# A hybrid attention block on one core: 128-row products in attention, a re-ordered start, and the last normalising turn inside the merge stage

## The chip, the cores and the metric

The kernel runs on one core of one Trainium2 chip. The metric is the device time of one execution in microseconds (us), lower is better. The core has five engines with a queue of their own each: TensorE (PE, with its weight loads as PEld), VectorE (DVE), ScalarE (ACT), GpSimd (POOL) and SyncE (SP); here SP issues most transfers. They wait for each other through semaphores.

## The reference: what is computed

A residual block over 2048 tokens of width 1024. A combined projection of the normalised input gives queries, keys, values and gates of two attention branches: FoX, 8 heads of 64, causal, with a cumulated forget term, and SWA, 8 query and 2 key heads in a sliding window with a distance penalty and a sink. Their outputs are gated, projected, merged and projected again.

```python
h = _rms_norm(x, norm_g[layer]) * (1.0 + scale[:, None, :]) + shift[:, None, :]
proj = h @ w_in[layer]
...
logits = logits + F[:, :, qs:qe, None] - F[:, :, None, :qe]
...
p = jax.nn.softmax(logits, axis=-1).astype(v.dtype)
...
logits = logits - slopes[:, :, None, None] * dist
...
p = jax.nn.softmax(jnp.concatenate([logits, sink], axis=-1), axis=-1)[..., :WK]
...
ya = (ya * jax.nn.silu(za)) @ w_o_fox[layer]
...
yb = (yb * jax.nn.silu(zb)) @ w_o_swa[layer]

merged = jax.nn.sigmoid(ga) * ya + jax.nn.sigmoid(gb) * yb
x = x + gate[:, None, :] * (merged @ w_out[layer])
```

The first two logits lines are FoX, the next two SWA.

## The kernel before

Five stages follow each other, each a block at whose end the engines meet: condition and norm, `project` (its last product ends near 1102 us), `attention` (to 1737 us), `merge` and `output`. Operands are held as a high and a low part, so that most products come as three.

**Attention** is a list of 350 steps, worked out before the kernel is built. A step is one 128-key tile of a FoX block (512 queries of a head; 32 blocks) or one part of an SWA unit (a tile of 128 queries, 4 heads; 32 units): part A over the current keys, part B over the 64 before them. `units` says how many SWA units stand inside each FoX block. In step n TensorE works on row maxima (`row_max`), then on the scores of step n+3 (`score`), then on the product of step n with the values (`gather`). ScalarE takes the exponential of the scores and casts it to its high part Ph, GpSimd subtracts for the low part Pl.

- FoX scores: L1266 multiplies Ka and Qa over HD + 4 = 68 rows (64 of the head, two for the forget term, two for the row maximum), L1267 the pair tiles Kb, Qb over 128 rows.
- `row_max` finds the shift of the softmax beforehand. For FoX it is L1028 (66 rows). For SWA L1037 puts the distance penalty (biasM) into the bank, and two products L1039 add QBa and KBa over HD = 64 rows; VectorE takes the maximum (L1095). Four such sets belong to one SWA tile; there are 16 tiles. The maxima go through a transpose and copies to two rows of Qa or QBa (`move_row`).
- SWA part B: L1277 and L1278 score, L1279 adds biasB over 64 rows, and L1307, L1308 and L1311 multiply Ph and Pl with VB over 64 rows.
- At its end each block is multiplied by its gate Z into yT (`collect`); the sums of the softmax go to memory (`copy_sums`), and eight turns read a group of them back, invert, store, load the inverses spread over all rows into R, and scale yT in four operations (`invert`, `scale`). The eighth turn comes behind the last step, in the `TAIL` of 28 empty steps.

**What sets the order.** `timed` gives each row maximum a due step, at least `TILE_LEAD` = 16 steps ahead of its block, and `at` the step in which it stands. `k_due`, `q_due`, `s_due` and `z_due` give the step at which SP issues the loads of keys, queries, SWA tiles and gates. SP works through its list in order: an entry that waits holds all behind it. `START` is -3. The maxima of the first three blocks are already made at the end of `project`. `tables` makes the 24 pieces of the bias tables on ScalarE in six steps from `TABLES_AT`; `set_up` fills constants on VectorE before its first step.

**Merge.** `split_rows` loads eight weight rows (512 KB each), ScalarE makes their high part (woh) and VectorE the low part (wol). yT is split in blocks of 256 tokens: ScalarE yh, GpSimd yl. TensorE's first product waits for the first block of yl and the first weight row, and VectorE gates the outputs with tiles of 1 MB each (`load_gates`).

## Time and profile before

| | us |
|---|---|
| time, median of 3 runs | 2129.09 (2123.26 to 2143.35) |
| the profiled execution | 2127.95 |
| its span, first to last instruction | 2126.2 |
| TensorE busy | 1979.7 (93%) |
| VectorE busy | 885.6 (42%) |
| ScalarE busy | 737.5 (35%) |
| GpSimd busy | 550.5 (26%) |

"Busy" of TensorE is the time in which a product is under way by the profile. Neighbouring products overlap there, so how fast TensorE works is read from the distance between starts. The granted clock is 1.00 at 2.4 GHz and 0.50 at 1.2 GHz; its mean over the span is 0.962.

### The profile page before, as it was taken

The numbers are of one execution on the slowest core, as the hardware profiler recorded it, in microseconds if no ns is written. First come the engines' busy times: TensorE is split into PE (matmuls) and PEld (weight loads), VectorE is DVE, ScalarE is ACT, GpSimd is POOL, SyncE is SP. The second block draws the span as 40 slices with busy tenths as digits, with TensorE's granted clock in tenths as the row PEclk, the third lists the DMA queues.
The fourth block names the chain that finished last, engine by engine and source line by source line (L and its number), as shares of the span: only waits on it lengthen the run. The fifth ranks groups of instructions, "written<-read, shape, count | busy, mean of one in ns | idle before, by whom it ended". The sixth has DMA issues, their size and how long they took to land. (4 is left out here: it accounts for less than half of the span.)

```text
span 2126.2 us, 27983 instructions
## 1 busy us (share of the span) xinstructions
PE 1979.7 (93%) x9722; PEld 1555.5 (73%) x9722; DVE 885.6 (42%) x1851; ACT 737.5 (35%) x1375; POOL 550.5 (26%) x502
## 2 busy tenths in 40 slices
PE   7389999999999999999989899999999959998998
PEld 2368778798788788888866566666666639997887
DVE  2945555562212220000234455555565335554332
ACT  2622222220112132121115677767777751002000
POOL 1600000000000000000004576767777742110000
PEclk9589999999999999999986999999999979999999
DMA  6233443345512212121424446446464334232322
GB/s 238 98 101 89 120 119 99 118 133 136 134 50 89 78 49 89 49 89 58 124 74 95 96 112 159 113 92 144 108 141 99 74 122 137 80 99 99 119 91 77
DMA packets 235435, 222.63 MB, mean 105 GB/s; under 512 B 54610, under 2 KB 188498, under 8 KB 234292
## 3 DMA queue, kind: packets, MB, share of 16 engines
q1 hardware_dynamic: 221892, 180.95, 30.8%
q0 software_dynamic: 11648, 39.85, 5.9%
q8 instruction: 55, 0.90, 0.2%
q10 hardware_dynamic: 1792, 0.53, 0.1%
q14 instruction: 48, 0.39, 0.1%
HBM read 149.18 MB, written 71.70 MB: 104 GB/s over the span
## 5 line engine op out<-in xcount | busy, mean ns | idle before, releaser
L1242 POOL TENSOR_TENSOR Pl<-PT,Ph 128x512 fp32r<-128x512 f32 (+2 forms) x350 | 415.5, 1204 | 200.2 <-ACT Ph L1342 192.9
L474 PE MATMUL pj<-hTh,Wh 128*128 128x512 f32 x768 | 299.6, 390 | 0.7 <-DVE Wl L679 0.4
L475 PE MATMUL pj<-hTl,Wh 128*128 128x512 f32 x768 | 299.0, 389 | 0.0
L476 PE MATMUL pj<-hTh,Wl 128*128 128x512 f32 x768 | 298.9, 389 | 0.0
L474 PE MATMUL pj<-Wh,hTh 128*128 128x512 f32 (+1 forms) x640 | 246.1, 385 | 23.9 <-DVE Wl L679 23.9
L376 POOL DMA_DIRECT2D wraw<-in_w_in x84 | 45.1, 537 | 856.4 <-DVE Wl L679 850.3
L1335 ACT ACTIVATE PT<-sc 128x512 f32<-128x512 f32 (+2 forms) x350 | 192.6, 550 | 137.7 <-PE sc L1267 46.2
L476 PE MATMUL pj<-Wh,hTl 128*128 128x512 f32 (+1 forms) x640 | 240.0, 375 | 0.0
L475 PE MATMUL pj<-Wl,hTh 128*128 128x512 f32 (+1 forms) x640 | 239.9, 375 | 0.0
L1342 ACT ACTIVATE Ph<-PT 128x512 fp32r<-128x512 f32 (+2 forms) x350 | 207.9, 594 | 11.2
L1082 DVE TENSOR_REDUCE part_max<-mx 128x1 f32<-128x512 f32 (+3 forms) x267 | 157.6, 599 | 98.4 <-PE mx L1028 97.1
L474 PEld LDWEIGHTS pj<-hTh,Wh 128*128 128x128 f32 x768 | 144.2, 188 | 33.6 <-DVE Wl L679 3.0
L679 DVE TENSOR_TENSOR Wl<-wraw,Wh 128x512 fp32r<-128x512 f32 x88 | 57.1, 689 | 263.3 <-ACT Wh L579 262.7
L476 PEld LDWEIGHTS pj<-hTh,Wl 128*128 128x128 f32 x768 | 144.1, 188 | 30.2
L475 PEld LDWEIGHTS pj<-hTl,Wh 128*128 128x128 f32 x768 | 144.2, 188 | 29.4
L474 PEld LDWEIGHTS pj<-Wh,hTh 128*128 128x128 f32 x640 | 121.6, 190 | 48.2 <-issue 17.0
L1028 PE MATMUL mx<-Ka,Qa 66*128 66x512 f32 (+2 forms) x296 | 119.6, 408 | 20.8 <-DMA Qb<-qk_scratch 9.8
L476 PEld LDWEIGHTS pj<-Wh,hTl 128*128 128x128 f32 x640 | 121.6, 190 | 21.8
L475 PEld LDWEIGHTS pj<-Wl,hTh 128*128 128x128 f32 x640 | 121.9, 191 | 19.1
L651 ACT ACTIVATE st<-pj 128x512 f32<-128x512 f32 x64 | 38.3, 598 | 272.6 <-PE pj L476 266.3
L1266 PE MATMUL sc<-Qa,Ka 68*128 68x512 f32 (+1 forms) x320 | 127.5, 398 | 1.7 <-ACT PT L1335 1.6
L1311 PE MATMUL ot<-Pl,V 128*65 128x512 f32 (+1 forms) x320 | 114.4, 374 | 12.2 <-POOL Pl L1242 12.1
(231 smaller groups left out, 3553.5 us busy)
## 6 DMA issues: line engine op xcount, KB each, us to landing
qk_scratch<-qThl SPq DMA_DIRECT2D x96, 256.0 KB, 2.8
wraw<-in_w_in POOLq DMA_DIRECT2D x88, 256.0 KB, 3.8
g_scratch<-st SPq DMA_DIRECT2D x64, 256.0 KB, 2.4
gt<-g_scratch SPq DMA_DIRECT2D x16, 1024.0 KB, 7.8
xin<-in_x POOLq DMA_DIRECT2D x16, 512.0 KB, 5.0
wada<-in_w_ada SPq DMA_DIRECT2D x8, 1024.0 KB, 7.7
z_scratch<-st SPq DMA_DIRECT2D x32, 256.0 KB, 2.4
Qb<-qk_scratch SPq DMA_DIRECT2D x32, 256.0 KB
```

The costliest lines, as they stand in the source:

```text
L376: pool.dma_start(wraw[k % RAW][:], io["w_in"][0, k * P:(k + 1) * P, bass.ds(col0, COLS)]).then_inc(w_in[k % RAW], 16)
L474: nc.tensor.matmul(out, a_hi, b_hi, start=first, stop=False)
L475: nc.tensor.matmul(out, a_hi, b_lo, start=False, stop=False)
L476: return nc.tensor.matmul(out, a_lo, b_hi, start=False, stop=last)
L679: nc.vector.tensor_tensor(Wl[:, k, :], wraw[k % RAW][:], Wh[:, k, :].bitcast(F32), ALU.subtract).then_inc(w_split, 1)
L1028: nc.tensor.matmul(bank[:, 0:w], Qa[i % NQ][0:HD + 2, a * P:(a + 1) * P], Ka[h % 2][0:HD + 2, c * QW:c * QW + w], start=True, stop=True).t ...
L1082: tr = nc.vector.tensor_reduce(part_max[:, t, c:c + 1], bank[:, 0:full], AX.X, ALU.max)
L1242: pool.tensor_tensor(Pl[n % NPH][0:rows, 0:w], PT[n % NP][0:rows, 0:w], Ph[n % NPH][0:rows, 0:w].bitcast(F32), ALU.subtract).then_inc(low_ ...
L1266: nc.tensor.matmul(bank[:, cols], Ka[h % 2][0:HD + 4, keys], Qa[u][0:HD + 4, q], start=cols.start == 0, stop=False)
L1311: mm = nc.tensor.matmul(part(slice(0, OUT)), values[:, HD:HD + OUT], low, start=False, stop=closing)
L1335: nc.scalar.activation(PT[n % NP][0:rows, 0:w], bank_s[n % NSC][0:rows, 0:w], ACT.Exp).then_inc(exp_done, 1)
L1342: nc.scalar.activation(Ph[n % NPH][0:rows, 0:w], PT[n % NP][0:rows, 0:w], ACT.Copy).then_inc(cast_done, 1)
```

## The change

1. **Rows.** The first FoX score product runs over all 128 rows: Ka holds ones and Qa zeros in the 60 rows added. The SWA maxima run over 66 rows instead of 64; the two added ones hold the shift of the tile two before (zero at first), which VectorE takes off again with one more operation. biasB and VB have 128 rows, the upper half zeros, and part B multiplies over 128. New fills in `set_up` and `maxima` write these constants, and TensorE waits for 13 `ready` marks instead of 8.
2. **Order at the start of attention.** The head of the list of maxima moves from step -3 to step 1, the tables from step 1 to 4, the first SWA units and loads later, the due step of SWA tile 2 from 16 steps ahead to 11. The first four FoX blocks hold 0, 0, 0, 4 SWA units instead of 0, 0, 1, 3.
3. **The end.** The last turn of sums and inverses moves into the merge stage (`Finish`), `TAIL` falls to 2, four of the eight weight rows are loaded while head 7 runs, and the first block of yT is split in halves. Z, R and tiles of merge and output lie elsewhere in memory.

```diff
-        units = ((0, 1, 1, 2) if i >= JB else (0, 0, 1, 3))[j]
+        units = ((0, 1, 1, 2) if i >= JB else (0, 0, 0, 4))[j]
...
+    READY = 13
...
-    TABLES_AT, TABLE_TURNS = 1, 6
+    TABLES_AT, TABLE_TURNS = 4, 6
...
-            due = min(start - TILE_LEAD, due)
+            due = min(start - (TILE_LEAD if (kind, i) != ("s", 2) else 11), due)
...
-    at = [None] * NU + [max(math.floor(due), START + u // 2) for u, (it, due) in enumerate(later)]
+    at = [None] * NU + [max(math.floor(due), 1 + u // 2) for u, (it, due) in enumerate(later)]
...
-    k_due = when(((h, c), START + 2 + 2 * c if h < 2 else last["f", (h - 2) * JB + 3] - AHEAD + 1 + 5 * c) for h in range(1, FOX_H) for c in range(JB))
-    q_due = when((i, START + i - NE + 1 if i < NQ else last["f", i - NQ] - AHEAD + 1) for i in range(NE, NB))
+    k_due = when(((h, c), START + 6 + c if h < 2 else last["f", (h - 2) * JB + 3] - AHEAD + 1 + 5 * c) for h in range(1, FOX_H) for c in range(JB))
+    q_due = when((i, START + 8 * (i - NE) if i < NQ else last["f", i - NQ] - AHEAD + 1) for i in range(NE, NB))
...
-    s_due = when((t, START + 1 + 7 * t if t < 2 else last["s", 2 * t - 3] + 1) for t in range(TT))
-    z_due = when((e, START + 2 + 2 * e if e < NZ else last[blocks[e - NZ]] + 2) for e in range(NBLK))
+    s_due = when((t, START + 4 + 11 * t if t < 2 else last["s", 2 * t - 3] + 1) for t in range(TT))
+    z_due = when((e, START + 1 + e if e < NZ else last[blocks[e - NZ]] + 2) for e in range(NBLK))
...
+    turns[-1] = NS + 1000
...
-    TAIL = 28
+    TAIL = 2
...
+    rooms = [nc.alloc_sbuf_tensor_at(f"w_o_early{k}", [P, 2, D], F32, offset=at) for k, at in enumerate((RAW_AT, HOT_AT))]
+    keep["early_rows"] = [room[:, m, :] for room in rooms for m in range(2)]
...
-    Z = [sb(f"Z{k}", [P, QW]) for k in range(NZ)]
+    Z = [sb(f"Z{k}", [P, QW], F32, ST_AT + 4 * QW * k) for k in range(NZ)]
...
-    R = sb("R", [P, 4, QW])
-    pick, rs = sb("pick", [HD + 4, OUT], F32R)[:], sb("rs", [P, 32])
+    R = sb("R", [P, 4, QW], F32, HOT_AT - 8192)
...
-    biasA, biasB = sb("biasA", [P, SWA_H, P], F32R), sb("biasB", [HD, SWA_H, CHUNK], F32R)
+    biasA, biasB = sb("biasA", [P, SWA_H, P], F32R), sb("biasB", [P, SWA_H, CHUNK], F32R)
...
-    VB = [sb(f"VB{k}", [HD, KV_H, VW], F32R) for k in range(2)]
+    VB = [sb(f"VB{k}", [P, KV_H, VW], F32R) for k in range(2)]
...
+                    pe.wait_ge(ready, READY)
...
-                mm = nc.tensor.matmul(out[:, k, :], QBa[i % 2][0:HD, h0 + k, :], KBa[i % 2][0:HD, a, off:], start=False, stop=k == 1)
+                mm = nc.tensor.matmul(out[:, k, :], QBa[i % 2][0:HD + 2, h0 + k, :], KBa[i % 2][0:HD + 2, a, off:], start=False, stop=k == 1)
...
-                st.settle(nc.vector.scalar_tensor_tensor(shift[:, i % 2, 0], top[:, i % 2], -1.0, sinks_neg[:], ALU.mult, ALU.min))
+                st.settle(nc.vector.tensor_tensor(top[:, i % 2], shift[:, i % 2, 0], top[:, i % 2], ALU.subtract))
+                st.settle(nc.vector.tensor_tensor(shift[:, i % 2, 0], top[:, i % 2], sinks_neg[:], ALU.min))
...
+    def load_weights(sp):
+        sp.wait_ge(scored, last["f", (FOX_H - 1) * JB - 1] + 1)
+        for k, tile in enumerate(keep["early_rows"]):
+            sp.dma_start(tile, io["w_o_fox"][0, k * P:(k + 1) * P, :]).then_inc(keep["w_o_in"][k], 16)
...
-            nc.vector.memset(Ka[0][HD:HD + 4, :].bitcast(F32), 1.0).then_inc(cleared, 1)
+            nc.vector.memset(Ka[0][HD:P, :].bitcast(F32), 1.0).then_inc(cleared, 1)
...
+                early_steps.settle(nc.vector.memset(Qa[k][HD:P, :].bitcast(F32), 0.0))
...
-                    if n == START:
+                    if n == START + 1:
                         load_q(sp, NE - 1, (1,))
-                    if n == START + 1:
+                    if n == last["f", (FOX_H - 1) * JB - 1] + 2:
+                        load_weights(sp)
...
-                        pe.wait_ge(ready, 8)
+                        pe.wait_ge(ready, READY)
...
-                            nc.tensor.matmul(bank[:, cols], Ka[h % 2][0:HD + 4, keys], Qa[u][0:HD + 4, q], start=cols.start == 0, stop=False)
+                            nc.tensor.matmul(bank[:, cols], Ka[h % 2][:, keys], Qa[u][:, q], start=cols.start == 0, stop=False)
...
-                        mm = nc.tensor.matmul(out, identr[0:rows, 0:rows], (biasA if x == "A" else biasB)[:, heads, :], start=False, stop=True)
+                        mm = nc.tensor.matmul(out, identr[:, 0:rows], (biasA if x == "A" else biasB)[:, heads, :], start=False, stop=True)
...
-                                  by_head(Ph[n % NPH][0:rows, 0:w]), by_head(Pl[n % NPH][0:rows, 0:w]))]
+                                  by_head(Ph[n % NPH][:, 0:w]), by_head(Pl[n % NPH][:, 0:w]))]
...
+                    st.settle(nc.vector.memset(Qa[k][HD:P, :].bitcast(F32), 0.0))
...
+                        nc.vector.memset(QBa[k][HD:HD + 2, :, :].bitcast(F32), 0.0).then_inc(ready, 1)
+                        nc.vector.memset(VB[k][HD:P, :, :].bitcast(F32), 0.0).then_inc(ready, 1)
+                    nc.vector.memset(biasB[HD:P, :, :].bitcast(F32), 0.0).then_inc(ready, 1)
...
+                    st.settle(nc.vector.memset(shift[:], 0.0))
...
-                    nc.vector.memset(Ka[1][HD:HD + 4, :].bitcast(F32), 1.0).then_inc(cleared, 1)
+                    nc.vector.memset(Ka[1][HD:P, :].bitcast(F32), 1.0).then_inc(cleared, 1)
...
+        ring = keep["early_rows"] + [spare[:, c:c + D] for c in range(2 * D, 2 * KT * TB, D)]
+        load, high, low, w_split = split_rows(nc, ctx, "m", sources, ring, Wh, Wl, keep["w_o_in"])
...
+            finish.sums(sp)
...
+            finish.inverses(sp)
...
+            low_y(0, 0, slice(BK, KT))
+            finish.wait(pool)
+            low_y(0, 1, slice(0, KT))
...
-            pe.wait_ge(y_split, 1)
...
+                if k == BK:
+                    pe.wait_ge(y_split, 1)
...
-            high_y(0, 0)
...
+            high_y(0, 0, slice(0, BK))
+            high(act, 0)
+            high_y(0, 0, slice(BK, KT))
+            for k in range(1, KT):
...
+            dve.wait_ge(y_hi, 1)
+            nc.vector.tensor_tensor(yl[0][:, 0:BK, :], yT[:, 0:BK, 0:TB], yh[0][:, 0:BK, :].bitcast(F32), ALU.subtract)
...
+                if k == 1:
+                    finish.invert(dve)
...
+            gate(0, 0, range(BK))
+            finish.scale(dve)
+            gate(0, 0, range(BK, KT))
+            gate(0, 1)
```

Three places in the order of instructions. First TensorE from the start of attention (mx is the bank of a maximum, sc of a score, ot of an output; the digit behind a name counts its buffers). Before:

```order
L1028 MATMUL mx0<-Ka0_670,Qa3_677 128x512
L1028 MATMUL mx1<-Ka0_670,Qa3_677 128x512
L1266 MATMUL sc0<-Qa0_674,Ka0_670 128x512
L1267 MATMUL sc0<-Qb0_679,Kb0_672 128x512
L1269 MATMUL sc0<-identr_665,maskr_664 128x128
L1028 MATMUL mx2<-Ka0_670,Qa3_677 128x512
L1028 MATMUL mx0<-Ka0_670,Qa3_677 128x128
```

After:

```order
L1328 MATMUL sc0<-Qa0_676,Ka0_672 128x512
L1329 MATMUL sc0<-Qb0_681,Kb0_674 128x512
L1331 MATMUL sc0<-identr_665,maskr_664 128x128
L1328 MATMUL sc1<-Qa0_676,Ka0_672 128x384
L1329 MATMUL sc1<-Qb0_681,Kb0_674 128x384
L1331 MATMUL sc1<-identr_665,maskr_664 128x128
L1328 MATMUL sc1<-Qa0_676,Ka0_672 128x128
L1329 MATMUL sc1<-Qb0_681,Kb0_674 128x128
L1331 MATMUL sc1<-identr_665,maskr_664 128x128
L1328 MATMUL sc2<-Qa0_676,Ka0_672 128x256
```

The maxima on query tile 3 have moved behind the first gather; the stage begins with scores of query tile 0.

Second the sync queue further on, where SWA tile 1 (QBa1 to VB1) is loaded. Before:

```order
L1192 DMA Z0_697<-z_scratch 64x512
L980 DMA Ka1_671<-qk_scratch 64x512
L988 DMA Kb1_673<-qk_scratch 128x512
L1176 DMA QBa1_707<-qk_scratch 64x8x128
L1176 DMA QBb1_709<-qk_scratch 128x8x128
L1176 DMA KBa1_711<-qk_scratch 64x2x192
L1176 DMA KBb1_713<-qk_scratch 128x2x192
L1177 DMA VA1_715<-v_scratch 128x2x128
L1179 DMA VB1_717<-v_scratch 64x2x128
```

After:

```order
L988 DMA Ka1_673<-qk_scratch 64x512
L996 DMA Kb1_675<-qk_scratch 128x512
L1005 DMA Qa1_677<-qk_scratch 64x512
L1007 DMA Qb1_682<-qk_scratch 128x512
L1260 DMA Z1_700<-z_scratch 64x4x128
L1244 DMA QBa1_709<-qk_scratch 64x8x128
L1244 DMA QBb1_711<-qk_scratch 128x8x128
L1244 DMA KBa1_713<-qk_scratch 64x2x192
L1244 DMA KBb1_715<-qk_scratch 128x2x192
L1245 DMA VA1_717<-v_scratch 128x2x128
L1247 DMA VB1_719<-v_scratch 64x2x128
```

Tile 1 stood behind the gate Z0; now it stands behind the reload of query tile 1 and the gate Z1, whose load waits for two collected blocks.

Third ScalarE at the start of merge. Before:

```order
L1573 ACTIVATE yh0<-yT 128x2048
L1471 ACTIVATE woh<-w_raw0 128x1024
L1471 ACTIVATE woh<-w_raw1 128x1024
L1471 ACTIVATE woh<-gt1 128x1024 x4
L1471 ACTIVATE woh<-w_raw0 128x1024
L1471 ACTIVATE woh<-w_raw1 128x1024
L1573 ACTIVATE yh1<-yT 128x2048
```

After:

```order
L1637 ACTIVATE yh0_17382<-yT 128x1024
L1523 ACTIVATE woh_17378<-w_o_early0_670 128x1024
L1637 ACTIVATE yh0_17382<-yT 128x1024
L1523 ACTIVATE woh_17378<-w_o_early0_670 128x1024
L1523 ACTIVATE woh_17378<-w_o_early1_671 128x1024 x2
L1523 ACTIVATE woh_17378<-gt1_17381 128x1024 x2
L1523 ACTIVATE woh_17378<-w_o_early0_670 128x1024 x2
L1637 ACTIVATE yh1_17383<-yT 128x2048
```

The first copy of yT (L1573, now L1637) is halved, weight row 0 stands between the halves, and the first four rows come from tiles that are loaded in attention.

## Rows read from the trace of the kernel before

**Rows 1.** TensorE's waits: waiter and who it waited for, total us, times, longest.
```profile
PE pa L1538 <- DVE wol L1475: 23.5, 1, 23.5
...
PE ot L1311 <- POOL Pl L1242: 12.1, 25, 0.7
...
PE mx L1028 <- DMA Qb<-qk_scratch: 9.8, 1, 9.8
...
PE mx L1037 <- DMA VB<-v_scratch: 6.2, 1, 6.2
...
PE mx L1037 <- ACT biasB L1328: 3.2, 1, 3.2
```

**Rows 2.** Windows: length, busy PE, PEld, DVE, ACT, POOL, clock, DMA, GB/s.
```profile
1112.00:1120.00 8.00, 8.00 (x25) 6.20 (x25) 5.96 (x12) 3.97 (x8) 3.24 (x3) 0.50 1.02 214
1132.00:1158.00 26.00, 25.26 (x67) 16.52 (x67) 7.35 (x24) 11.19 (x25) 9.71 (x9) 0.50 0.35 62
1184.00:1192.00 8.00, 5.46 (x14) 3.46 (x14) 1.66 (x5) 1.23 (x2) 1.06 (x2) 0.50 0.43 94
1196.00:1690.00 494.00, 473.41 (x2275) 320.97 (x2274) 276.64 (x702) 365.37 (x697) 349.20 (x295) 1.00 0.50 116
```

**Rows 3.** Timeline of TensorE, one set of SWA maxima: start, duration (us).
```profile
1302.70 0.34 PE L1037 MATMUL mx<-biasM,identr 128*128 128x384 f32 x1
1302.97 0.47 PE L1039 MATMUL mx<-KBa,QBa 64*128 64x192 f32 x2
1303.37 0.50 PE L1266 MATMUL sc<-Qa,Ka 68*128 68x512 f32 x1
1303.70 0.39 PE L1267 MATMUL sc<-Qb,Kb 128*128 128x512 f32 x1
1303.94 0.40 PE L1307 MATMUL ot<-Ph,V 128*65 128x512 f32 x1
```

**Rows 4.** Timeline of TensorE: scoring a part B, and gathering one.
```profile
1274.82 0.28 PE L1278 MATMUL sc<-QBb,KBb 128*64 128x256 f32 x1
...
1275.57 0.39 PE L1308 MATMUL ot<-Ph,V 128*64 128x512 f32 x1
...
1300.56 0.28 PE L1267 MATMUL sc<-Qb,Kb 128*128 128x128 f32 x1
1300.67 0.27 PE L1269 MATMUL sc<-identr,maskr 128*128 128x128 f32 x1
...
1301.60 0.28 PE L1267 MATMUL sc<-Qb,Kb 128*128 128x256 f32 x1
```

**Rows 5.** Groups by line and shape, TensorE: count, busy us, mean ns.
```profile
L1039 PE MATMUL mx<-KBa,QBa 64*128 64x192 f32 x120 | 29.3, 325 | 0.0
...
L1307 PE MATMUL ot<-Ph,VB 64*65 64x256 f32 x30 | 9.9, 330 | 0.0
```

**Rows 6.** Timeline at the start of attention: SP, TensorE, VectorE.
```profile
1105.19 0.33 SPq L999 DMA_DIRECT2D Qb<-qk_scratch  x1
...
1111.55 0.76 PE L1028 MATMUL mx<-Ka,Qa 66*128 66x512 f32 x1 [9.83 <-DMA Qb<-qk_scratch]
1111.61 1.76 DVE L1401 MEMSET Ka<- 4x2048 f32 x1 [0.38 <-issue]
```

**Rows 7.** Timeline: first load of SWA tile 2, and TensorE's use of it.
```profile
1178.70 0.58 SPq L1176 DMA_DIRECT2D QBa<-qk_scratch  x1
...
1186.54 0.66 PE L1037 MATMUL mx<-biasM,identr 128*128 128x384 f32 x1 [6.16 <-DMA VB<-v_scratch]
```

**Rows 8.** Timeline from the end of attention into merge.
```profile
1721.72 0.33 PE L1311 MATMUL ot<-Pl,V 128*65 128x256 f32 x1 [0.41 <-POOL Pl L1242]
...
1737.74 1.91 ACT L1573 ACTIVATE yh<-yT 128x2048 fp32r<-128x2048 f32 x1 [15.06 <-DVEq L1585]
...
1739.84 4.50 POOL L1531 TENSOR_TENSOR yl<-yT,yh 128x2048 fp32r<-128x2048 f32 x1 [18.17 <-ACT yh L1573]
...
1751.06 1.23 DVE L1475 TENSOR_TENSOR wol<-w_raw,woh 128x1024 fp32r<-128x1024 f32 x1
```

150 lines of the change are left out of this document (90 added, 60 removed).

## The prediction

> **What bounds the kernel now.** I read the list of TensorE's waits first, then busy time by window, then the attention stage instruction by instruction. The waits [rows 1] say that TensorE has few long ones: 23.5 us between attention and merge, 9.8 us between projection and attention, 6.2 us on VB and 3.2 us on biasB, both early in attention. The largest of the small ones is GpSimd: 12.1 us in 25 waits. The windows [rows 2] add two things. In the long middle of attention, 1196 to 1690 us, TensorE is busy 473.4 of 494.0 us at clock 1.00, GpSimd 349.2 and ScalarE 365.4, so TensorE sets the pace. And the clock was at its lower level (0.50, which is 1.2 GHz) for 1112 to 1120 and all of 1132 to 1158 us, although TensorE was busy 8.00 of 8.00 and 25.26 of 26.00 us. A page of busy shares hides the third thing, which only start times show: "busy" in the middle is not all columns. That is the largest term below.
>
> **Term A, products over 64 rows.** In the timeline [rows 3] one set of SWA maxima stands between products over more rows. L1267, over 128 rows, begins 0.33 us after L1266, but a 512-column product needs 0.23 to 0.24 us from start to start elsewhere (1303.70 to 1303.94, the next rows). From the start of L1037 to that of L1267 it is 1303.70 - 1302.70 = 1.00 us. What it should be: 384 columns at 0.23 per 512 is 0.175; two products of 192 columns are held at 0.11 each by their 128-column weight loads (0.11 is the distance of the 128-column products in [rows 4], 1300.56 to 1300.67); 512 columns are 0.235. Sum 0.63. So 0.37 us is lost at each set, where the row count goes from 128 to 64 and back. L1266, with 68 rows, stands next to 128-row products without any such loss: it is the 64 that costs, and from 66 rows on nothing is lost in any row I read. The change makes these products 66 rows deep.
> The steps on the half window ("B") show the same twice [rows 4]. Gathering over VB (64 rows): from L1269 at 1300.67 to L1267 at 1301.60, 0.93 us, where 128 columns (0.11 or less) and four times 256 (0.117 each) need 0.58: 0.35 lost. Scoring, with biasB over 64 rows: from L1278 at 1274.82 to L1308 at 1275.57, 0.75 us, where 256 + 256 + 512 columns need 0.47: 0.28 lost. After the change both run over 128 rows.
> Counts [rows 5]: 120 products of 192 columns make 60 sets; some 56 of them lie in the warm part. 56 x 0.37 = 20.7; 30 x 0.35 = 10.5; 30 x 0.28 = 8.4; together 39.6 us. Not all of it will be kept: the engines behind have less slack (GpSimd goes from 349/494 = 71% to 349/455 = 77%), and its 12.1 us of waits will grow. I take off a tenth: **A = -35.5**. Bounds: -40 if all is kept, 0 if depth was not the cause.
> The Trainium skill, "TensorEngine Tiling (Array Packing)", section Key Properties, says "Changing tiling mode (not just tile) drains the TensorE", and its list of modes has 64-row and 128-row ones; 66 rows would fall in the latter. Another of its pages, "TensorE: Matmul & The Clock Gate", section LDWEIGHTS, says that the number of rows does not matter to a weight load, only its columns; by that alone A would be 0 and the sum 35.5 us worse. The 0.37 us of rows 3 speaks for the first.
>
> **Term B, the first product of each FoX step over 128 rows, and the opening.** Going from 68 to 128 rows costs nothing: L1266 (68) and L1267 (128) have the same distance to the next, and weights of 128 columns either way. What it can do is to the clock: it loads more of the array in the stretches at 0.50. At half speed 1112 to 1120 and 1132 to 1158 us lose (8 + 26)/2 = 17 us.
> The opening itself is re-ordered. Before, the stage's queues start at 1105.19 [rows 6] and TensorE at 1111.55, since its first instruction is a FoX row maximum on a query tile not yet loaded (the 9.8 us wait in [rows 1], of which the 6.2 after the stage's start can go). After, it is a score whose tiles are all there: -6.2. The bias tables are made three steps later, but the first SWA maxima come four steps later: -3.2, the biasB wait.
> Two new waits take its place. First, VectorE fills more before it takes a maximum. It ended at 1111.61 + 1.76 = 1113.4 [rows 6], with a fill of 2048 columns. Added are fills of 2 x 512 (Qa), 2 x 1024 (QBa), 2 x 264 (VB) and 512 columns (biasB), 4112 in all: 4112 / 2048 x 1.76 = 3.5 us, so 1116.9. TensorE, cold from 1105.3, has three scores and two gathers to do first and stands at its fourth maximum at about 1112.5; it waits some 4.5 to 5 us for the bank. Second, on the sync queue the loads of SWA tile 1 now stand behind the load of Z1 that waits for the second block's output (y_done 2, FoX block 1, collected in step 10), and TensorE wants tile 1 in step 11. Such a load of six transfers took from 1178.70 to 1186.54 = 7.8 us [rows 7]; about 2 us of work covers it, so a wait of about 6 us.
> Each of the two lets the clock fall again, as every long wait did. Three wake-ups of about 4.5 us (the stretch from 1186.54 [rows 7] was back at full clock by about 1192) lose 7 us, against 17 before: -10. Sum: -6.2 - 3.2 + 5 + 6 - 10 = **-8.5**. Bounds: -20 without the new waits, +4 if the clock stays down as long as before.
>
> **Term C, the load of SWA tile 2.** Its 6.2 us wait came since the maxima followed the load by a step or two. Now the load is issued after step 28, and the maxima stand in step 32: 3 steps of about 1.4 us cover 4 to 5 of the 7.8 us. A wait of 3 us stays, short enough, I think, for the clock to hold; before, 1184 to 1192 was at 0.50, 5.5 us of it busy. -6.2 + 3 - 2.3 = **-5.5**; bounds -9 and 0.
>
> **Term D, the end of attention.** Before [rows 8]: the last product ends at 1721.72 + 0.33 = 1722.05; then sums to memory and back, inverses to memory and back, four multiplications, and only then the merge stage: ScalarE's copy of yT at 1737.74, TensorE at 1722.05 + 23.5 = 1745.6 [rows 1]. After, that last turn runs inside merge, and four of the eight weight rows lie there already. The new chain: about 1.2 us to collect the last block and change stage, half a yT copy (1.91/2 = 0.95), the copy of weight row 0, as many columns (0.95), its low part (1.23), and some 0.6 in hand-overs: 4.9 us, say 5. So -18.5. The low parts of yT, on VectorE and GpSimd, lie beside it. It can come back later: the inverses' transfer is now behind two 1 MB gate loads, and four multiplications on VectorE (2048 columns, 2 x 1.23 = 2.5) and GpSimd's low part of block 1 (4.50) follow it. TensorE wants that part when it has done block 0, 8 x 24 = 192 products of 256 columns at 0.117 = 22.5 us and some 3.5 for the cold start and the gates' arrival, so 31 us after attention's last product. I guess the inverses landed at 24: 24 + 2.5 + 4.5 = 31, just level, so I give back 1. **D = -17.5**; bounds -19 and -10.
> At nothing: the 2 MB of weight rows loaded during head 7 (its FoX keys and values are there by then; DMA is at 0.50 in that window) and one more small VectorE operation per SWA tile (VectorE 276.6 of 494 us).
>
> **Sum.** -35.5 - 8.5 - 5.5 - 17.5 = -67.0. The profiled execution took 2127.95 us (span 2126.2), 1.1 below the median of the runs shown: 2127.95 - 67.0 = 2060.95; I say **2061**.
>
> **Rivals.**
> R1, the depth was not the cause: the SWA sets stay at 1.00 us, A = 0. 2061 + 35.5 = 2096.5. Against it: the loss shows at each of the three 64-row places and at no 66- or 68-row one. Chance 0.08.
> R2, another engine takes over: with TensorE quicker, steps of five 512-column products (5 x 0.233 = 1.17 us) are no longer than GpSimd's mean tile (349.2/295 = 1.18 us [rows 2]), so GpSimd or the row loads eat another third of A: 2061 + 12 = 2073. For it: the 25 waits on GpSimd. Against: a step with a maximum is 1.40 us, and three steps of lead smooth it. Chance 0.15.
> R3, the early waits just move: the opening keeps the clock down as long as before and tile 2 waits as long: B = +4, C = 0, 2061 + 12.5 + 5.5 = 2079. Chance 0.12.
> R4, the tail comes back in merge: D = -10, 2061 + 7.5 = 2068.5. Chance 0.08.
> R5, better than said: the clock wakes early and stays: B = -20, 2061 - 11.5 = 2049.5. Chance 0.07.
> R6, slower than before: more of the array loaded lowers the granted clock in attention. The stage would have some 560 us of work at full clock; it decides from 67/560 = 0.12 more time, a mean clock under 0.89; at 0.80 the time would be 2061 + 560 x 0.25 = 2201. Against it: four of the five products of a FoX step run over 128 rows already, and the window of 494 us is at 1.00 [rows 2]. Chance 0.02.
> R7, faster by little: A = 0 and B and half of D gone too, 2061 + 35.5 + 8.5 + 8.5 = 2113.5: 0.03.
> The forecast itself: 0.45.
>
> **Numbers.** The range takes in the forecast, R2, R3, R4 and R5 and leaves out R1, R6, R7: 2043 to 2088. About 1% (21 us) is what a measurement of this kernel can tell from no change. Faster by over 1% are all but R6 and R7: 0.95; same 0.03; slower 0.02.
>
> **What would show it.** A: in the new timeline the maxima set of three products and the next score take about 0.63 us, and the middle of attention is about 35 us shorter with the same counts. B: first attention product about 6 us earlier after the stage's start; a wait on VectorE near the fourth maximum; one on SWA tile 1's load, and fewer windows at 0.50. C: a wait of 3 us or less at tile 2. D: about 5 us between last attention and first merge product. I am wrong if the sets still take 1.00 us, if waits on GpSimd in attention exceed 25 us, or if the clock stays at 0.50 for over 20 us again.

## The result, and the profile after

The changed kernel takes 2101.81 us (median of 4 runs, 2100.4 to 2106.73) where the kernel before took 2126.59 beside it: a ratio of 0.9863, 95% interval 0.9818 to 0.9907. It is faster, by 25 us and not by 67, and outside the range of the prediction. The profiled execution has a span of 2100.8 us where the one before had 2126.2.

The list of TensorE's waits after the change, to be held against [rows 1]. Columns: engine and line that waited, what released it, total us, times, longest us.

```profile
engine line waited for: us in total, times, longest us
...
PE mx L1036 <- DVE shift_rows L1085: 18.0, 18, 4.4
PE ot L1373 <- POOL Pl L1304: 13.5, 27, 0.9
...
PE mx L1046 <- DMA VB<-v_scratch: 12.1, 2, 8.4
PE mx L1036 <- DMA Ka<-qk_scratch: 11.8, 6, 2.9
...
PE mx L1036 <- DVE part_max L1091: 7.2, 1, 7.2
...
PE pa L1601 <- DVE yT L1668: 5.6, 2, 3.9
PE pa L1601 <- DVE wol L1527: 5.3, 2, 4.9
PE sc L1328 <- PEq L323: 3.7, 1, 3.7
PE sc L1339 <- DMA QBa<-shift_rows: 3.3, 1, 3.3
...
PE mx L1046 <- ACT biasB L1390: 0.6, 1, 0.6
```

The 23.5 us ahead of merge are 4.9 now, the 3.2 on biasB are 0.6. GpSimd, which the prediction feared, went from 12.1 only to 13.5. But shift_rows went from 7.0 to 18.0, Ka from 3.8 to 11.8 and VB from 6.2 to 12.1, and part_max is new.

Term A's place in the timeline after, to be held against [rows 3]: the set of SWA maxima and the score behind it.

```profile
1303.38 0.34 PE L1046 MATMUL mx<-biasM,identr 128*128 128x384 f32 x1
1303.56 0.36 PE L1048 MATMUL mx<-KBa,QBa 66*128 66x192 f32 x2
1303.76 0.42 PE L1328 MATMUL sc<-Qa,Ka 128*128 128x512 f32 x1
1304.02 0.40 PE L1329 MATMUL sc<-Qb,Kb 128*128 128x512 f32 x1
```

From L1046 to L1329 it is 0.64 us, as forecast (0.63); before it was 1.00. So the mechanism is right. What takes its place is in the same trace three microseconds later.

```profile
1300.93 0.33 SPq L1119 DMA_DIRECT2D rs<-sums  x1
1301.30 1.28 SPq L988 DMA_DIRECT2D Ka<-qk_scratch  x1
...
1304.89 0.58 SPq L1129 DMA_DIRECT2D inv<-rs  x1
1305.52 0.70 SPq L988 DMA_DIRECT2D Ka<-qk_scratch  x1
...
1307.37 0.27 PE L1023 MATMUL mx<-ident,nmax 128*4 128x128 f32 x1
...
1309.08 0.26 ACT L1055 ACTIVATE shift_rows<-mx 4x128 fp32r<-4x128 f32 x1
1309.44 0.28 DVE L1085 TENSOR_TENSOR shift_rows<-mx,shift_rows 4x128 fp32r<-4x128 f32 x1 [2.14 <-ACT shift_rows L1055]
...
1310.52 0.30 PE L1036 MATMUL mx<-Ka,Qa 66*128 66x128 f32 x1 [2.88 <-DMA Ka<-qk_scratch]
```

Two chains end at 1310.52. SyncE issues the fourth key load of the next head behind a turn of the sums, at 1305.52, five microseconds ahead. And ScalarE copies the row that TensorE transposed at 1307.37 only at 1309.08; the bank is free when VectorE has followed.

A second place shows why ScalarE is late.

```profile
1160.26 3.20 ACTq L1069 DMA_DIRECT2D QBa<-shift_rows  x4
...
1163.51 0.27 ACT L1055 ACTIVATE shift_rows<-mx 4x128 fp32r<-4x128 f32 x1 [2.63 <-issue]
...
1164.21 0.80 PE L1036 MATMUL mx<-Ka,Qa 66*128 66x512 f32 x1 [4.45 <-DVE shift_rows L1085]
```

ScalarE's sequencer (ACTq) issues the four transfers that move a row of SWA maxima into QBa; that takes 3.20 us, and copies and exponentials stand behind it. The page counts none of this as busy. In the windows below ScalarE shows 358.68 of 484 us; its 56 issues at L1069, of 0.63 us each by the median, and its 52 at L1063, of 0.60, are 68 us more.

Windows after (busy us per engine, with the granted clock third from the end of a row), to be held against [rows 2]:

```profile
1104.00:1112.00 8.00, 7.39 (x28) 5.75 (x28) 7.07 (x14) 6.25 (x11) 4.91 (x10) 0.66 0.74 193
1112.00:1120.00 8.00, 1.36 (x4) 1.07 (x5) 6.53 (x21) 0.00 (x0) 1.15 (x1) 0.76 0.80 167
...
1136.00:1144.00 8.00, 0.73 (x4) 0.42 (x3) 1.90 (x8) 2.40 (x4) 2.52 (x2) 0.54 0.71 172
1144.00:1152.00 8.00, 6.68 (x25) 5.33 (x26) 2.20 (x7) 2.46 (x4) 1.50 (x2) 0.60 0.04 9
...
1192.00:1200.00 8.00, 8.00 (x27) 6.11 (x28) 3.03 (x8) 3.23 (x6) 2.56 (x2) 0.62 0.00 1
1216.00:1224.00 8.00, 4.39 (x14) 2.70 (x14) 1.81 (x3) 5.59 (x11) 4.54 (x5) 0.66 1.14 216
1196.00:1680.00 484.00, 443.13 (x2261) 321.79 (x2260) 286.87 (x712) 358.68 (x690) 342.87 (x292) 0.98 0.53 122
```

The clock is low for less time than before, as forecast, but TensorE stands idle instead: 1.36 of 8 us busy at 1112, 0.73 of 8 at 1136. The rows of these two stops, and the sync queue between them:

```profile
1117.89 1.29 DVE L1091 TENSOR_REDUCE part_max<-mx 128x1 f32<-128x512 f32 x2
1118.64 0.48 PE L1036 MATMUL mx<-Ka,Qa 66*128 66x128 f32 x1 [7.25 <-DVE part_max L1091]
...
1136.88 0.63 SPq L1260 DMA_DIRECT2D Z<-z_scratch  x1
1137.55 0.65 SPq L1244 DMA_DIRECT2D QBa<-qk_scratch  x1
...
1145.32 0.66 PE L1046 MATMUL mx<-biasM,identr 128*128 128x384 f32 x1 [8.41 <-DMA VB<-v_scratch]
```

And the end, against [rows 8]:

```profile
1716.95 0.58 PE L1601 MATMUL pa<-yh,woh 128*128 128x256 f32 x1 [4.95 <-DVE wol L1527]
...
1732.35 0.38 PE L1601 MATMUL pa<-yh,woh 128*128 128x256 f32 x1 [1.71 <-DVE yT L1668]
...
1748.05 0.55 PE L1601 MATMUL pa<-yh,woh 128*128 128x256 f32 x1 [3.93 <-DVE yT L1668]
```

VectorE and GpSimd ahead of the last of these waits (the four scalings, a gating operation, the low part of the second block of yT):

```profile
1740.53 2.50 DVE L1145 TENSOR_TENSOR yT<-yT,R 128x512 f32<-128x512 f32 x4 [4.86 <-DMA R<-inv]
...
1743.72 4.17 DVE L1668 TENSOR_TENSOR yT<-ta,tb 128x256 f32<-128x256 f32 x1
```

```profile
1743.10 4.51 POOL L1587 TENSOR_TENSOR yl<-yT,yh 128x2048 fp32r<-128x2048 f32 x1 [23.97 <-DVE yT L1145]
```

### The profile page after: what moved, and what is told of

The parts are those of the page before. It is cut to its first block and busy times, and to the rows that moved or that the text cites. A ratio compares the mean times of both kernels' runs of the same rounds, so it can differ in the third digit from the quotient of the medians.

```text
span 2100.8 us, 27959 instructions
## 1 busy us (share of the span) xinstructions
PE 1941.9 (92%) x9722; PEld 1553.0 (74%) x9722; DVE 907.9 (43%) x1879; ACT 733.0 (35%) x1376; POOL 547.9 (26%) x502
## 5 line engine op out<-in xcount | busy, mean ns | idle before, releaser
L1404 ACT ACTIVATE Ph<-PT 128x512 fp32r<-128x512 f32 (+2 forms) x350 | 207.9, 594 | 11.1
L474 PEld LDWEIGHTS pj<-hTh,Wh 128*128 128x128 f32 x768 | 144.1, 188 | 33.5 <-DVE Wl L679 2.9
L1328 PE MATMUL sc<-Qa,Ka 128*128 128x512 f32 (+1 forms) x320 | 125.3, 392 | 6.0 <-PEq L323 3.7
L1373 PE MATMUL ot<-Pl,V 128*65 128x512 f32 (+1 forms) x320 | 113.9, 372 | 13.8 <-POOL Pl L1304 13.5
```

The source lines that it names most:

```text
L474: nc.tensor.matmul(out, a_hi, b_hi, start=first, stop=False)
L1328: nc.tensor.matmul(bank[:, cols], Ka[h % 2][:, keys], Qa[u][:, q], start=cols.start == 0, stop=False)
L1373: mm = nc.tensor.matmul(part(slice(0, OUT)), values[:, HD:HD + OUT], low, start=False, stop=closing)
L1404: nc.scalar.activation(Ph[n % NPH][0:rows, 0:w], PT[n % NP][0:rows, 0:w], ACT.Copy).then_inc(cast_done, 1)
```

## A balance of the middle

To size term A in every kernel I took the same piece of work, from ScalarE's exponential of step 60 to that of step 340, and split TensorE's time there by its timeline. "Columns" prices each product at 0.2333 us per 512 columns (the distance of the 512-column products), at least 0.107 for one under 256 columns. "Waits" are the idle times that the profile names. "Other" is the rest: switches of the row count, stretches at the lower clock, short gaps. Some records are missing from a trace, so a line is good to about 1 us as a reading. Each kernel was profiled in one execution, though: five kernels from below that leave the order of work in this piece as it is (u_end, u_fox, u_start, a_sdue, a_lead8) take 453.3, 456.2, 454.2, 455.0 and 448.6 us in it, where the changed kernel takes 452.4.

| kernel | rows | piece | columns | waits | other |
|---|---|---|---|---|---|
| before | 64 | 464.1 | 400.7 | 20.6 | 42.6 |
| after | 66/128 | 452.4 | 400.3 | 34.9 | 17.0 |
| u_rows | 64 | 464.2 | 400.9 | 21.4 | 41.8 |
| b_rows | 66/128 | 455.7 | 400.9 | 35.0 | 19.7 |
| c_start_64 | 64 | 450.6 | 401.4 | 11.1 | 37.8 |
| c_start | 66/128 | 438.0 | 400.6 | 25.6 | 11.6 |
| e_turn_64 | 64 | 430.3 | 401.6 | 1.4 | 27.0 |
| e_turn | 66/128 | 417.2 | 401.0 | 13.4 | 2.5 |
| b_kmt | 64 | 431.7 | 401.6 | 1.9 | 28.0 |
| e_act | 66/128 | 438.8 | 400.2 | 26.6 | 11.9 |
| e_open | 66/128 | 410.8 | 401.1 | 11.6 | -2.2 |

The loss at the 64-row places alone can be had from the same traces, since a product that stands beside them starts later than its neighbour's columns ask for. Summed over the 48 sets and 25 parts B of the piece and without the stretches at the lower clock, the rows take 32 to 33 us off these places in three of the four pairs (before and b_rows, u_rows and after, e_turn_64 and e_turn) and 31 in the fourth. "Other" falls by less, 23 to 26, because it also takes in 3 to 6 us of products at the lower clock and up to 4.5 us of short gaps that come with the rows.

## Experiments

Each ran beside the kernel before; the ratio to it is given with its interval, 0.2% to 0.5% (4 to 10 us) to each side. The changed kernel itself was measured once, beside 2126.59 us; beside the later kernels the kernel before took 2128.44 to 2131.17. Differences to the changed kernel below are of medians and carry this shift: by the ratios, the 9 us of u_start are 6, the 8 and 7 us of a_kearly and a_moves are 6 and 5, and nothing under 5 us is told from zero.

**Undoing or adding one part.** u_rows puts the 64 rows back:

```diff
-QBa[i % 2][0:HD + 2, h0 + k, :], KBa[i % 2][0:HD + 2, a, off:]
+QBa[i % 2][0:HD, h0 + k, :], KBa[i % 2][0:HD, a, off:]
-identr[:, 0:rows] ... (VA or VB)[t % 2][:, g, :] ... Ph[:, 0:w], Pl[:, 0:w]
+identr[0:rows, 0:rows] ... (VA or VB)[t % 2][0:rows, g, :] ... Ph[0:rows, 0:w], Pl[0:rows, 0:w]
```

> The changed kernel with the SWA maxima and part B back over 64 rows; biasB, VB and their fills keep their 128 rows in memory. By the prediction's term A (0.37, 0.35 and 0.28 us at 56, 30 and 30 places) the 64 rows cost 35.5 us: about 2137 us. Theory S (ScalarE, with the transfers that it issues, is the next bound: busy and issuing 441.7 of 494.0 us in the middle of attention before, 434.6 of 484.0 after) says that only part of the 39.6 us was ever to be had: 10 to 20 us, so 2112 to 2122, and TensorE's waits on shift_rows and Pl shrink again to the values of the kernel before (in the trace after, shift_rows 18.0 us in 18 waits). If the row count was not the cause: no change, 2102.

2127.86 us, ratio 0.9997 (0.997 to 1.0024): 26 us slower than the changed kernel. The rows are the largest part of the gain, more than theory S gave them and less than the prediction did. The two profiled executions differ by 19 us only, 11.8 of them in the piece above and 9.2 ahead of it, from the first exponential to that of step 60. Its waits went back:

```profile
PE mx L1036 <- DVE shift_rows L1085: 8.7, 14, 2.9
...
PE mx L1036 <- DMA Ka<-qk_scratch: 5.0, 6, 1.4
```

b_rows is the same edit the other way round, put into the kernel before.

> The kernel before with the rows of the SWA maxima (66) and of part B (128) alone, its order of work and its end as they were; FoX stays at 68 rows. The prediction's term A: 2126.6 - 35.5 = 2091, or 4 us more for the fills at the start. Theory S: ScalarE has 494.0 - 441.7 = 52 us free in the middle, of which its waits need some; gain 10 to 20 us, so 2107 to 2117, with longer waits on shift_rows, Ka and Pl than before (3.8, 4.2 and 7.3 us in the 369 us from 1293 us on).

2111.07 us, 0.9917 (0.9892 to 0.9942): 19 us faster than before and inside theory S's range, with waits on shift_rows of 13.9 us and on Ka of 13.0. The rows bring these waits by themselves.

u_fox (`Ka[h % 2][0:HD + 4, keys], Qa[u][0:HD + 4, q]` again):

> The changed kernel with the first FoX score product back over 68 rows (the fills stay). The prediction: no change at full clock, 2102 +- 3. If the 128 rows help TensorE's clock where it falls, this kernel shows more windows at the lower clock and is 3 to 10 us slower; if more rows in work lower the clock (the dips to 0.83 in 1306 to 1316, 1376 to 1386 and 1456 to 1466 us of the trace after), the dips vanish here and it is about 5 us faster.

2105.43 us, 0.9893 (0.9845 to 0.9942): 4 us slower at most, not resolved. The windows from 1120 to 1128 us stand at 0.50 here and at 0.81 in the changed kernel; the later ones do not differ in one direction. Whether the 128 rows of this product help the clock stays open.

u_start puts the order of the start back:

```diff
-(0, 0, 0, 4)            TABLES_AT = 4   max(math.floor(due), 1 + u // 2)     START + 4 + 11 * t
+(0, 0, 1, 3)            TABLES_AT = 1   max(math.floor(due), START + u // 2) START + 1 + 7 * t
...
```

> The changed kernel with the order of the start as before: units, the places of the first maxima, tables, and the loads of keys, queries, SWA tiles and gates. By the prediction's terms B (order part) and C it should be 8.5 + 5.5 = 14 us slower: 2116. By the traces, where the exponential of step 50 came 1 us later after than before, it should be the same or 1 to 3 us faster, since the waits of 7.2, 8.4 and 4.4 us at 1118, 1145 and 1164 us took what the new order gave: 2098 to 2102.

2092.62 us (2089.92 to 2096.42), 0.9837 (0.9789 to 0.9884): 9 us faster than the changed kernel, whose own runs begin at 2100.4. The new order was a loss, even against what the traces had made me expect; c_start below finds the same, by 11 us, between two kernels that were measured together. From the first exponential to that of step 60 the kernel before takes 128.8 us, the changed one 139.3, u_start 124.0. The new order starts TensorE 6 us earlier (3.7 us after its last product in `project`, where it was 9.8 and, in u_start, 10.0) and gives back 15.

u_end puts the last turn back behind attention (`TAIL = 28`, nothing left to `Finish`); the four early weight rows stay.

> The changed kernel with the last turn of sums, inverses and scaling back behind the last step of attention (28 empty steps); the four early weight rows stay. By the prediction's term D, 17.5 us slower, of which the four early rows may carry some: 2117 to 2119. If the chain of sums did not set the end but the weight rows did, under 5 us slower.

2114.81 us, 0.9924 (0.9903 to 0.9945): 13 us slower, less than expected. Its wait ahead of merge is 19.0 us instead of 4.95, and its largest wait on yT 1.7 instead of 3.93.

**What ate the rest of term A.** a_kearly loads the next head's keys sooner, b_moves and a_moves let SyncE issue the row transfers:

```diff
-last["f", (h - 2) * JB + 3] - AHEAD + 1 + 5 * c
+last["f", (h - 2) * JB + 3] - AHEAD + 1 + 2 * c
...
 (ScalarE's loop)
-                    for kind, i in row_move(n):
-                        move_row(act, kind, i)
 (SyncE's loop, ahead of k_due)
+                    for kind, i in row_move(n):
+                        move_row(sp, kind, i)
```

> The changed kernel with the four key loads of heads 2 to 7 issued two steps apart instead of five, so that all four stand ahead of the turn of the sums in SyncE's order (in the trace after the fourth was issued at 1305.52 us, and TensorE waited until 1310.52 for it). Rival K: the 11.8 us of waits on Ka go and with them the dips of the clock to 0.83 (some 5 us): 10 to 15 us faster, 2087 to 2092. Theory S: the same wait has ScalarE's late copy of the row behind it (the copy at 1309.08 us for a transpose that ran at 1307.37), so 0 to 5 us faster, the wait renamed shift_rows.

2093.59 us, 0.9836 (0.9786 to 0.9886), 8 us faster, between the ranges of the two theories. There is no wait on Ka left in its list, and the piece above shortens by 8.6 us. Both theories had a half: the keys were a cause, and shift_rows rose from 18.0 to

```profile
PE mx L1036 <- DVE shift_rows L1085: 19.6, 24, 4.2
```

> The changed kernel with the transfers that move the row maxima into Qa and QBa issued by SyncE instead of ScalarE (only those of attention's own steps; the three early ones stay). They take ScalarE 32.1 + 37.8 = 69.9 us in 1196 to 1680 us of the trace after. Theory S: ScalarE is the next bound and its four issues of some 3 us at an SWA tile hold the row copies and exponentials behind them; TensorE's waits on shift_rows (18.0 us) and part of those on Pl (13.5) go, and those at 1164 and 1220 us (4.4, 3.3): 15 to 25 us faster, 2077 to 2087. Rival K (the next head's keys come late): 0 to 5 us faster, the waits on Ka stay at 10 us or more. Rival Q: SyncE's queue, whose loads stand behind each other, brings the rows late: a new wait on Qa or QBa, slower.

2094.66 us, 0.984 (0.9795 to 0.9884), 7 us faster, less than theory S said. The waits on ScalarE and GpSimd went, and others took their place: the keys first, VectorE (7.6 us on part_max and 5.6 on nmax that the changed kernel does not have, but for 0.4), and QBa (7.4 for 3.3), as rival Q had it.

```profile
PE mx L1036 <- DMA Ka<-qk_scratch: 18.5, 6, 5.3
...
PE mx L1036 <- DVE shift_rows L1085: 2.4, 4, 1.5
PE ot L1375 <- POOL Pl L1306: 2.2, 5, 0.7
```

So GpSimd was not the main cause of the waits that carry its name: with the same subtractions, but rows and exponentials that come in time, 13.5 us became 2.2.

> The kernel before with only the transfers of the row maxima issued by SyncE instead of ScalarE. Theory S as refined: before the change TensorE itself (with its losses at 64 rows) set the pace, and ScalarE had 52 us free, so little comes: 0 to 6 us faster, 2121 to 2127, and a_moves gains much more than this. If it gains as much as a_moves, ScalarE's issues held both kernels alike and are not where term A went.

2125.08 us, 0.9973 (0.9942 to 1.0003): 6 us or nothing, as expected.

c_km has both edits, c_start also the old start.

> The changed kernel with both: key loads of heads 2 to 7 two steps apart, and the row transfers issued by SyncE. Alone they gave 8.0 and 7.0 us (2093.6 and 2094.7 against some 2102), and each left the other's wait: keys early left 19.6 us on shift_rows and 13.4 on Pl, the row transfers on SyncE raised the waits on Ka from 11.8 to 18.5. If these two are the two things that kept term A from its full size, together they give more than the sum, 18 to 25 us: 2077 to 2084. If there is a third limit of the same size (VectorE, which holds its reductions for 5.6 + 7.6 us in the run with the row transfers on SyncE), 10 to 15 us: 2087 to 2092.

> The same two edits, and also the order of the start as before. The old order gave 9 us alone (2092.6). If the start and the middle add up: 9 us under c_km, 2068 to 2075, and faster than both kernels. If the old order's gain came from the middle (another spacing of the SWA units), nothing is added to c_km.

2083.15 us, 0.9783 (0.9748 to 0.9818), and 2072.59, 0.973 (0.9695 to 0.9766). Together they give 19 us, the lower end of the first branch, and the old start 11 more: parts add up. The limit that the rival named is there as well, though not at its price: TensorE waits 12.1 us on nmax and 9.3 on part_max ahead of the SWA maxima in c_km. In c_start's timeline:

```profile
1424.73 0.48 SPq L1119 DMA_DIRECT2D rs<-sums  x1
...
1433.93 0.35 DVE L1133 RECIPROCAL rs<-rs 128x32 f32<-128x32 f32 x1 [9.10 <-DMA rs<-sums]
...
1435.30 0.37 PE L1023 MATMUL mx<-ident,nmax 128*4 128x128 f32 x1 [6.21 <-DVE nmax L1100]
```

A load of 16 KB, issued with query and gate loads around it, is used 9.2 us later; VectorE waits with the maxima behind it, and TensorE with VectorE. In the changed kernel that reciprocal waited 0.2 us in all; the new places of the loads brought it.

> c_start with the SWA maxima and part B back over 64 rows. The difference to c_start is what the rows are worth once the waits on keys and on ScalarE are taken away. Undone in the changed kernel they were worth 26 us, added to the kernel before 19 us. If the missing part of the 35.5 us went into those two waits: 32 to 38 us slower than c_start. If the loss at 64 rows was itself over-counted (fewer places, or cover by other waits): 24 to 28 us, as before.

2100.54 us, 0.9875 (0.984 to 0.991), 28 us slower than c_start: the number of the "24 to 28" branch, but not its reason, since the places lost what was counted (see the balance). The two profiled executions differ by 17.5 us.

e_turn sets the turns later:

```diff
-invert n + 4, inv_store n + 5, inv_load n + 8,  scale n + 13 + 3 * m
+invert n + 7, inv_store n + 8, inv_load n + 11, scale n + 17 + 2 * m
```

> c_start with each turn of the sums set later against its load: inversion 7 steps behind the turn instead of 4, store 8 instead of 5, load of the inverses 11 instead of 8, scalings at 17, 19, 21, 23 instead of 13, 16, 19, 22. In c_start VectorE stood 22.3 us in three waits at the reciprocal (the longest 9.1 us, the load of 16 KB issued at 1424.73 and used at 1433.93), and TensorE behind it 13.7 us on nmax and 7.4 on part_max. If that is the third limit: both waits fall under 3 us each and the time by 12 to 18 us, 2055 to 2061. If the next thing in SyncE's queue takes over (row transfers late, a wait on QBa): 0 to 5 us, 2068 to 2073.

> e_turn with the SWA maxima and part B back over 64 rows. The difference to e_turn is what the rows are worth when keys, row transfers and turns no longer hold TensorE. Counted by the prediction's places: 39.6 us. In c_start it was 28 us (2100.5 against 2072.6), where the waits on nmax and part_max were 10.8 us longer than over 64 rows. If those waits took the rest: 34 to 42 us. If the places lose less than counted: 24 to 30 us again.

2054.38 us, 0.9631 (0.9606 to 0.9656), 18 us faster than c_start; with 64 rows 2069.14, 0.971 (0.9694 to 0.9726). The rows are worth 15 us here, which no branch had. How the 26, 19, 28 and 15 us of the four pairs differ among each other should not be read closely: executions of one kernel lie up to 14 us apart, and the profiled ones differ by 19, 10, 18 and 15. That all are under 35.5 the balance explains. Over 64 rows e_turn waits 1.4 us in the piece, over 66 and 128 rows 13.4, the longest on the keys again (3.2 us) and on VectorE (2.2). Each of the four pairs in the table says the same: the rows take 23 to 26 us from "other" (24.8, 22.9, 26.2, 24.5) and put 12.0 to 14.5 into "waits". The quicker TensorE catches up with whatever is next, every time, and by about the same amount whether ScalarE issues the row transfers or SyncE.

**The start.** a_sdue moves the load of SWA tile 1 ahead (`START + 4 + 6 * t`), a_lead8 the maxima of tile 2 back (8 for 11), e_open is e_turn with the changed kernel's start and a_sdue's load.

> The changed kernel with the load of SWA tile 1 issued at step 7 instead of 12, which puts it ahead of the load of Z that waits for the second block's output. If that Z load is what held tile 1 (8.4 us of TensorE's time at 1145 us), the wait falls to under 2 us and the clock stays up there: 8 to 12 us faster, 2090 to 2094. If the time only moves to the next wait of the opening (4.4 us at 1164, 3.7 at 1192, 3.3 at 1221 us), 0 to 4 us faster.

2099.09 us, 0.987 (0.9831 to 0.9909): the waits on VB fall from 12.1 to 6.6 us, but the time by 3 us at most. In the traces the stretch from the first exponential to that of step 60 is 7.2 us shorter (132.1 for 139.3); where the rest of that went is not settled.

> The changed kernel with the maxima of SWA tile 2 due 8 steps ahead of its first step instead of 11, three more steps behind its load. The prediction's term C had a wait of 3 us with the clock held; it measured 3.7 us with the clock at its lower level behind it. If that wait pulled the clock down: it goes, and 5 to 8 us come (2094 to 2097). If the row transfers then come late for the tile's score (3.3 us at 1220.90 before), that wait grows by as much and nothing comes: 2100 to 2103.

2099.18 us, 0.9861 (0.9839 to 0.9883): the wait on tile 2 is gone, and the one on QBa is longer,

```profile
PE sc L1339 <- DMA QBa<-shift_rows: 9.6, 1, 9.6
```

where it was 3.3. The time lies between the two branches, nearer the second, whose reason this is.

> e_turn with the changed kernel's order of the start, and the load of SWA tile 1 at step 7 as in a_sdue. By the waits: the new order starts TensorE about 8 us earlier, then waits 8.1 us on VectorE's fills, 3.2 on tile 1, 3.5 on shift_rows (ScalarE's transfers, gone here), 3.4 on tile 2, 3.8 on QBa; the old order waits 10.0, 4.4, 3.3, 6.3 and 1.7 us. If the new order was slower only for the waits on tile 1 and on ScalarE's transfers, this is as fast as e_turn or up to 4 us faster. If its starting point (TensorE stopped twice within 50 us, the clock falling each time) is the loss: 4 to 9 us slower than e_turn.

2053.4 us, 0.9642 (0.9625 to 0.9658), as fast as e_turn. So the new order is no loss by itself. With ScalarE's transfers gone and tile 1 still behind Z it was one of 11 us (c_km and c_start); how much of the mending is tile 1's and how much the later turns' no pair of runs separates.

**ScalarE's transfers, and how much was there before.** e_act is e_open with the row transfers back on ScalarE; b_kmt is the kernel before (its rows, start and end) with keys, row transfers and turns mended.

> e_open with the row transfers back on ScalarE: the changed kernel with tile 1 loaded at step 7, keys early and the turns later. Theory S: ScalarE's issues hold the row copies; the waits on shift_rows (13 us between the exponentials of steps 60 and 340 in a_kearly) and Pl (11) are back, and it is 14 to 22 us slower than e_open (2053.4): 2067 to 2075. If moving them only mattered through the turn: under 6 us slower, 2053 to 2059.

2082.71 us, 0.9795 (0.9749 to 0.9841): 29 us slower than e_open, from that alone, and more than theory S said; 28.0 us of it lie in the piece of the table. There ScalarE works or issues for 412.4 of 438.8 us (94%) in e_act and for 366.7 of 410.8 (89%) in e_open; its issues are 89.0 and 19.9 us of that. Before the change it was 416.6 of 464.1 (90%). The busy share of 74% in [rows 2] did not show it. But the share with the issues is no full account either: e_open at 89% waits 11.6 us, the kernel before at 90% lost at most 6 us by its transfers (b_moves). What e_open lacks is the runs of two or four issues, up to 3.2 us long, with copies and exponentials behind them; that the runs cost and not the sum of the issues was not tested by itself. The list of TensorE's waits in e_act:

```profile
PE mx L1036 <- DVE shift_rows L1085: 17.0, 24, 4.1
PE ot L1373 <- POOL Pl L1304: 14.4, 29, 0.9
```

The Trainium skill says of this, in "DMA: Bandwidth & Descriptors", section "Issuing engines are not separate DMA queues", that starting transfers from several engines saves only sequencer time, "which is usually small relative to the DMA itself". How it compares with these small transfers no run shows, but here it is the time that counts: 0.60 to 0.63 us of an engine that had 10% free.

> The kernel before, with its 64 rows, its start and its end, and the three edits around TensorE: keys early, row transfers by SyncE, turns later. Between the exponentials of steps 60 and 340 the kernel before took 464.1 us (400.7 of columns, 20.6 of waits, 42.6 other); e_turn_64 took 430.3 (401.6, 1.4, 27.0). If those three edits are what made that difference in the kernel before too, it falls to about 430 here, and the time by 30 to 36 us: 2095 to 2101, with no change of the rows at all. If they only work together with the changed start and end: 0 to 15 us, 2116 or more. b_moves alone gave 6.

2081.41 us, 0.9771 (0.9726 to 0.9816): 47 us faster than before without a single row changed, and 20 us faster than the change under study. That is more than the 30 to 36 expected. The piece came as said (431.7 us, 32 less); in the traces another 10.8 us lie between the first exponential and that of step 60, which the expectation left out. Between the two kernels "waits" fall by 18.7 us and "other" by 14.6. Of the latter some 2 us are a stretch at the lower clock behind a wait on Ka in the kernel before (0.50 from 1384 to 1387 us), some 6 stand right behind the 44 named waits, of which 4 are left, and the rest are gaps too short to be listed, whose cause I have not settled. b_moves without keys and turns gave 6.

## Why the prediction was wrong, step by step

**Where the time went.** The two profiled executions differ by 25.4 us. Up to attention's first exponential the changed kernel is 8.6 us earlier (1.6 of it in the stages before, which this change does not touch); from there to the exponential of step 60 it gives back 10.5. The middle is 11.7 us shorter. The stretch from attention's last product to merge's first is 18.6 us shorter, and the merge stage then 3.3 longer. So the opening, where terms B and C (-14) and a share of term A stood in the sum, cost 3.5 us; the middle gained a third of its share of term A, and the end nearly what was said.

**Term A, -35.5: the step that failed is "I take off a tenth".** The mechanism and the price of the places hold. By the working, the piece of the balance has 48 x 0.37 + 25 x (0.35 + 0.28) = 33.5 us to gain. Its 48 sets took 0.40 us more than their columns before and 0.02 after, scoring a part B 0.29 and 0.00, gathering one 0.31 and -0.02: 48 x 0.38 + 25 x (0.29 + 0.33) = 33.7 us went, also where a set is followed by another row maximum (0.36 to 0.37 each, against 0.39 ahead of a full FoX score). Yet the piece shortened by 11.7. What the prediction gave back to the engines behind, a tenth (4 us of 39.6), was about two thirds: 14.3 us came back as named waits (20.6 to 34.9), some 3 as products at the lower clock behind them (three stretches instead of one), and 4 as short gaps. The working looked at GpSimd's busy share and never at ScalarE's, since 74% looked free; its issues are not in that share. And it priced no load: at 1310 us the last keys were 2.88 us late where before they were 0.66. The four pairs show that neither is the one cause: with both mended the rows still brought back 12.0 us of waits.

Undone in the changed kernel the rows were worth 26 us, added to the kernel before 19.

**Term B, -8.5, and C, -5.5: the sign was wrong**; their order part was +9 by u_start (+6 by the ratios). By the times that is a miss of 20 us or more, the largest of a term, and the step that failed is the size and number of the waits that the new order brings. The single gains came: the first product 6.1 us earlier after the stage's start (said 6.2; 0.3 us after the sync queue's first load for 6.4), biasB 3.2 to 0.6, and the slow stretches cost less: busy time times the missing clock from 1104 to 1160 us gives 17 us before and 7 after, as forecast. The two waits that I named came larger, 7.2 for 5 and 8.4 for 6. Of the first, the fills are the cause: VectorE was done with them 14.4 us after the stage's start, 8.2 before, so they took 6.2 us more and not 3.5. Two that I had not named came too: 4.4 us at 1164 behind ScalarE's four issues, and 3.3 at 1221 on the row of tile 2, which follows its maxima by the same queue. I had asked what is queued behind the waits on SyncE, but not what ScalarE's queue does when the maxima move closer to their use. For C the wait on the load was as said (3.7 for 3), but the clock did fall (0.62 in 1192 to 1200 us); that it would hold had my own rows against it, where the 3.2 us wait on biasB ended at 1132.7 and 1132 to 1158 us stood at 0.50. a_lead8 shows that the wait's time only moves on to QBa. (The terms of B add up to -8.4, not -8.5, which changes nothing.)

**Term D, -17.5:** right in mechanism. From attention's last product to the first of `output` the trace has 220.7 us before and 205.4 after, 15.3 less; u_end, which keeps the four early weight rows, measures 13 for the turn alone. Ahead of merge it was 4.95 us, as worked out (5). The second block of yT came 3.9 us late where I gave back 1. The scalings (2.50 us) and the low part (4.51) were as said; the inverses were there 28.5 us after attention's last product and not 24. A gating operation on VectorE beside the low part took 4.17 us, where its neighbours take 0.42, and ended last (1747.89, the low part 1747.61).

**The rivals.** I had treated them as exclusive and centred the range on the case in which none of them happens. R2 (another engine takes a third of A, +12) came in about its size by the times (u_rows leaves 9.5 us of A out, b_rows 17) and well past it in the middle of the traces; and it came from ScalarE, the keys and VectorE instead of GpSimd. R3 (B +4, C 0) came in its number and past it, but not in its mechanism: the clock was low for less time, and the waits grew instead. R4 (the tail comes back, +7.5) came by 2 to 4.5 us. Added up in full the three give 2061 + 12 + 18 + 7.5 = 2098.5, 3 us from the result; that it is so near is in part luck, since the parts miss in both directions. R1, R6 and R7 did not come: the 64 rows cost, and the middle was at 0.98.

## What to carry to other kernels

Ahead of pricing a quicker TensorE, list what each microsecond saved runs into: the loads with the time from their issue to their use, and each engine's busy time with the transfers it issues, above all where several stand in a row. Here the loss was priced right to 1 us, from one place of each kind, and yet in none of the four pairs did more than 13 us of some 33 reach the time of the middle. Mending those limits first was worth more (47 us) than the rows. And when several small rivals rest on different places, add them: they do not exclude each other.
